# The last layer norm of a decoder layer: statistics by token on partitions, means and affines dealt out anew

## What is computed

```python
def layer_norm(x, g, b):
    mu = mean(x); var = mean((x - mu) ** 2)
    return (x - mu) * rsqrt(var + 1e-5) * g + b

h = silu(x @ w_ffn_gate) * (x @ w_ffn_up)
x = layer_norm(ALPHA * x + h @ w_ffn_down, ln_ffn_g, ln_ffn_b)
```

## Time and profile before

| | us |
|---|---|
| median of 3 runs | 2103.23 (2102.51 to 2103.74) |
| the profiled execution, its own time | 2103.31 |
| its span in the trace | 2101.7 |
| from tile 15 written (end of the last L2242) to the last affine's end | 2086.12 to 2098.58 |
| issue of the last store to the end of the span | 2099.0 to 2101.7 |

### The profile page before, as it was taken

How to read it: one execution, slowest core, us unless ns; L and a number is a source line. 1 busy time by engine, 2 the same in 40 slices (tenths; PEclk the granted TensorE clock), 3 DMA queues, 4 the chain that set the end, 5 groups by cost and what they waited for, 6 DMA issues and landing times.

```text
span 2101.7 us, 47661 instructions
## 1 busy us (share of the span) xinstructions
PE 2082.1 (99%) x17400; PEld 2065.5 (98%) x17400; DVE 1479.6 (70%) x2395; ACT 1117.4 (53%) x1671; POOL 161.8 (8%) x298
## 2 busy tenths in 40 slices
PE   9999999999999999999999999999999999999997
PEld 8999999999999999999999999999999999999997
DVE  8788877888698988544546876977666666545545
ACT  5566556566545545434434565656666665433333
POOL 1000000000002432000000000001111110000000
PEclk9999999999999999999999999999999999999998
DMA  7555555455567998555556575568888887555553
GB/s 279 195 180 180 191 193 185 159 185 188 184 200 236 319 293 281 182 183 180 180 186 204 193 283 194 164 223 285 278 293 286 277 283 256 176 190 182 181 183 110
DMA packets 125362, 451.78 MB, mean 215 GB/s; under 512 B 16056, under 2 KB 16312, under 8 KB 124232
## 3 DMA queue, kind: packets, MB, share of 16 engines
q1 hardware_dynamic: 101232, 366.41, 51.1%
q0 software_dynamic: 24048, 84.20, 12.9%
HBM read 427.87 MB, written 23.99 MB: 215 GB/s over the span
## 4 chain that ended last, share of the span: by engine, by line
PE 94%; DVE 3%; DMA 1%; ACT 1%; issue 0%; SPq 0%; ACTq 0%; POOL 0%; DVEq 0%
PE G L443 26%; PE G L444 26%; PE G L445 26%; PE M L443 4%; PE M L444 4%; PE M L445 4%; DVE sb_wlo L1482 1%; PE M L593 1%; PE M L605 1%; DMA sb_hist<-in_hist 1%; DMA sb_raw<-in_wstream 1%; DVE sb_resid L1770 0%; ACT sb_whi L953 0%; PE M L596 0%; PE M L576 0%
## 5 line engine op out<-in xcount | busy, mean ns | idle before, releaser
L1482 DVE TENSOR_TENSOR sb_wlo<-sb_raw,sb_whi 128x1024 fp32r<-128x1024 f32 x688 | 833.5, 1223 | 553.9 <-ACT sb_whi L953 550.2
L953 ACT ACTIVATE sb_whi<-sb_raw 128x1024 fp32r<-128x1024 f32 x688 | 720.7, 1057 | 733.7 <-PE G L445 612.9
L443 PE MATMUL G<-sb_xH,sb_whi 128*128 128x264 f32 (+1 forms) x3040 | 860.1, 283 | 2.2 <-DVE sb_wlo L1482 1.8
L445 PE MATMUL G<-sb_xH,sb_wlo 128*128 128x264 f32 (+1 forms) x3040 | 858.3, 282 | 0.0
L444 PE MATMUL G<-sb_xL,sb_whi 128*128 128x264 f32 (+1 forms) x3040 | 857.4, 282 | 0.0
L443 PEld LDWEIGHTS G<-sb_xH,sb_whi 128*128 128x128 f32 x3040 | 570.5, 188 | 4.6 <-DVE sb_wlo L1482 2.7
L444 PEld LDWEIGHTS G<-sb_xL,sb_whi 128*128 128x128 f32 x3040 | 570.1, 188 | 0.0
L445 PEld LDWEIGHTS G<-sb_xH,sb_wlo 128*128 128x128 f32 x3040 | 570.0, 188 | 0.0
L443 PE MATMUL G<-sb_hH,sb_whi 128*128 128x264 f32 x704 | 199.5, 283 | 0.0
L444 PE MATMUL G<-sb_hL,sb_whi 128*128 128x264 f32 x704 | 199.3, 283 | 0.0
L445 PE MATMUL G<-sb_hH,sb_wlo 128*128 128x264 f32 x704 | 198.0, 281 | 0.0
(11 more groups left out here) (389 smaller groups left out, 2975.8 us busy)
## 6 DMA issues: line engine op xcount, KB each, us to landing
sb_raw<-in_wstream SPq DMA_DIRECT2D x688, 512.0 KB, 4.2
sb_st<-in_state_ssd POOLq DMA_DIRECT2D x32, 512.0 KB, 6.4
out_new_ssd_s<-sb_st POOLq DMA_DIRECT2D x32, 512.0 KB, 3.9
sb_tmp<-in_state_ssd POOLq DMA_DIRECT2D x34, 256.0 KB, 4.8
...
```

Source lines behind the costliest of these rows:

```text
L443: pe.matmul(out, w, kH, start=start, stop=False)
L445: return pe.matmul(out, wlo[:, slot, at:at + P], kH, start=False, stop=stop)
L953: act.activation(hi, src, ACT.Copy).then_inc(hi_ready, 1)
L1482: dve.tensor_tensor(lo, src, hi.bitcast(F32), ALU.subtract)\
```

## The change

The same sums are made, but the statistics of the last norm lie by token: token on partitions, three columns (tokens 0 to 127, 128 to 255, and the last 128, of which the samples are the last eight rows). So the chain of variance, root and reciprocal runs on 128x3 values. The reciprocals come back to all partitions as a product of ones with a diagonal matrix. In detail:

- PE (`last_sums`): of x the sum to all partitions stays (two matmuls, L756); for both sums there are besides 12 matmuls with a sums tile as the stationary operand and one column of ones as the moving one (`by_token`, L760), each giving 128x1. Where the sum of squares was made for all partitions is nothing now.
- DVE: six operations of 3 or 6 columns (L2305 to L2315), ACT's root on 3 columns (L1480). Then DVE builds the diagonal `rdiag` (128x256 and 128x8, L2316, L2319), PE multiplies (`last_norm`, L787), DVE copies the result from PSUM to SBUF (`RSTD[2]`, L2324). ACT's square of the mean (L1446) is gone.
- Means: DVE takes it from pair 0, POOL from pairs 1 to 5 (five, not four), PE from pairs 6 and 7: the tile times the identity plus the mean times minus the identity, in PSUM (L778, L782).
- `scaled` takes `RSTD[2]` in SBUF as its second operand, and for pairs 6 and 7 the PSUM tiles as its first. The order is 0, 1, 6, 2, 7, 3, 4, 5.
- Affines: ACT has 12 tiles (pairs 0, 1, 6, 2, 7, 3), DVE four (4, 5). The stores go in the order 0, 1, 6, 2, 4, 7, 3, 5.
- One DVE operation more, 128x128, at the start of the last projection (`minus`).
- Five semaphores of the step that makes dt become two counters, `dt_vec` and `dt_act`: waits and increments stay on the same instructions.

```diff
--- before.py
+++ after.py
@@ -212,6 +212,9 @@
 OUT_SETS = (1, 0, 2)
+LAST_BY_ACT = (0, 1, 6, 2, 7, 3)
+LAST_BY_DVE = (4, 5)
+LAST_STORES = (0, 1, 6, 2, 4, 7, 3, 5)
 OUT_PAIRS = (1, 0, 2)
@@ -368,6 +371,8 @@
             outer=([P, 2, XPG, P],))
+        spare = outer[:, :, :, :].rearrange("p b i n -> p (b i n)")
+        rdiag, minus, tok = spare[:, 0:T], spare[:, T:T + P], spare[:, T + P:T + P + 9]
         (cols,) = overlay(2 * UNIT * 4, cols=([P, 2, 2, 2],))
...
@@ -420,12 +425,12 @@
                     load(i * RING, k)
-            for c in range(8):
-                if c < 7:
-                    sp.wait_ge(s["xn_ready"], 16 + c + 1)
+            for p in LAST_STORES:
+                if p in LAST_BY_ACT:
+                    sp.wait_ge(s["xn_ready"], 16 + LAST_BY_ACT.index(p) + 1)
                 else:
-                    sp.wait_ge(s["zn_ready"], 16)
-                sp.dma_start(o["yT"][:, c * 2 * T:(c + 1) * 2 * T], flat(resid[:, 2 * c:2 * c + 2, :]))\
+                    sp.wait_ge(s["zn_ready"], 8 + len(LAST_BY_ACT) + LAST_BY_DVE.index(p) + 1)
+                sp.dma_start(o["yT"][:, p * 2 * T:(p + 1) * 2 * T], flat(resid[:, 2 * p:2 * p + 2, :]))\
                     .then_inc(s["y_out"], 16)
@@ -544,7 +549,7 @@
-                    pe.wait_ge(s["dt_ready"], 1)
+                    pe.wait_ge(s["dt_vec"], 3)
@@ -747,15 +752,43 @@
-                def add(k, tile, start=False, stop=False):
-                    return pe.matmul(STAT[2][k][:, 0:T], ones[:, :], tile, start=start, stop=stop)
-                for k in range(2):
-                    pe.wait_ge(s["dsum_ready"], 4 + k + 1)
-                    add(k, SUMS[2][:, k, 0, :], start=True)
+                def all_rows(tile, start=False, stop=False):
+                    return pe.matmul(STAT[2][0][:, 0:T], ones[:, :], tile, start=start, stop=stop)
+
+                def by_token(out, tile):
+                    for c, at in enumerate((0, P, T - P)):
+                        last = pe.matmul(out[:, c:c + 1], tile[:, at:at + P], ones[:, 0:1], start=True, stop=True)
+                    return last
+
+                pe.wait_ge(s["dsum_ready"], 5)
+                all_rows(SUMS[2][:, 0, 0, :], start=True)
+                by_token(M[1][:, 0:3], SUMS[2][:, 0, 0, :])
+                pe.wait_ge(s["dsum_ready"], 6)
+                by_token(M[1][:, 3:6], SUMS[2][:, 1, 0, :]).then_inc(s["tok_stats"], 1)
                 pe.wait_ge(s["res_ready"], 25)
-                add(0, resid[:, KT - 1, :], stop=True).then_inc(s["ln_sum"], 1)
+                by_token(M[3], resid[:, KT - 1, :]).then_inc(s["tok_stats"], 1)
                 pe.wait_ge(s["dsq_ready"], 25)
-                add(1, SQUARES[2][:, 1, 1, :], stop=True).then_inc(s["ln_sq"], 1)
+                by_token(G[1][1], SQUARES[2][:, 1, 1, :]).then_inc(s["tok_stats"], 1)
+                all_rows(resid[:, KT - 1, :], stop=True).then_inc(s["ln_sum"], 1)
+
+            def last_norm():
+
+                def copied(p):
+                    for j in range(2):
+                        pe.matmul(GP[p - 6][:, j, 0:T], ident[:, :], resid[:, 2 * p + j, :], start=True, stop=False)
+
+                def less_mean(p):
+                    for j in range(2):
+                        last = pe.matmul(GP[p - 6][:, j, 0:T], minus, MEAN[2][:, :], start=False, stop=True)
+                    last.then_inc(s["last_ps"], 1)
+
+                copied(6)
+                pe.wait_ge(s["diag_ready"], 1)
+                pe.matmul(M[2][:, 0:T], ones[:, :], rdiag, start=True, stop=True).then_inc(s["last_ps"], 1)
+                pe.wait_ge(s["mean_ready"], 3)
+                less_mean(6)
+                copied(7)
+                less_mean(7)
@@ -926,6 +959,7 @@
             last_sums()
+            last_norm()
             assert t["unit"].now() == N_UNITS, (t["unit"].now(), N_UNITS)
...
@@ -1442,12 +1476,12 @@
                 act.activation(SQUARES[2][:, 1, j, :], resid[:, KT - 2 + j, :], ACT.Square).then_inc(s["dsq_ready"], 1)
+            act.wait_ge(s["var_ready"], 3)
+            act.activation(tok[:, 3:6], tok[:, 3:6], ACT.Sqrt, bias=eps[:, 1:2]).then_inc(s["lsd_ready"], 1)
             act.wait_ge(s["ln_sum"], 3)
-            act.activation(RSTD[2][:, :], STAT[2][0][:, 0:T], ACT.Square, scale=1.0 / D_MODEL).then_inc(s["mean_ready"], 1)
             act.activation(MEAN[2][:, :], STAT[2][0][:, 0:T], ACT.Copy, scale=1.0 / D_MODEL).then_inc(s["mean_ready"], 1)
-            ln_sd(2)
-            for p in range(7):
-                act.wait_ge(s["zn_ready"], 8 + p + 1)
+            for n, p in enumerate(LAST_BY_ACT):
+                act.wait_ge(s["zn_ready"], 8 + n + 1)
                 for k in (2 * p, 2 * p + 1):
...
@@ -2214,6 +2248,7 @@
             dve.wait_ge(s["st_out1"], 16 * 16)
+            dve.tensor_scalar(minus, ident[:, :], -1.0, None, ALU.mult)
             for b in range(7):
@@ -2254,37 +2289,49 @@
-            def less_mean(p):
-                total = STAT[2][0][:, 0:T].rearrange("p (o t) -> p o t", o=1).to_broadcast([P, 2, T])
-                return mark(dve.scalar_tensor_tensor(out=two(p), in0=total, scalar=-1.0 / D_MODEL, in1=two(p),
-                                                     op0=ALU.mult, op1=ALU.add))
-
-            def scaled(p):
-                return dve.tensor_tensor(two(p), two(p), M[2][:, 0:T].rearrange("p (o t) -> p o t", o=1).to_broadcast([P, 2, T]),
-                                         ALU.mult)
-
-            ln_variance(2)
-            dve.wait_ge(s["mean_ready"], 4)
-            dve.wait_ge(s["res_ready"], 25)
-            less_mean(0)
+            def spread_two(v):
+                return v.rearrange("p (o t) -> p o t", o=1).to_broadcast([P, 2, T])
+
+            def scaled(p, src=None):
+                return dve.tensor_tensor(two(p), two(p) if src is None else src, spread_two(RSTD[2][:, :]), ALU.mult)
+
+            def affine(p):
+                for k in (2 * p, 2 * p + 1):
+                    last = dve.tensor_scalar(resid[:, k, :], resid[:, k, :], vcol("ln_ffn_g", k), vcol("ln_ffn_b", k),
+                                             ALU.mult, ALU.add)
+                last.then_inc(s["zn_ready"], 1)
+
+            dve.wait_ge(s["tok_stats"], 1)
+            step(dve.tensor_scalar(tok[:, 0:6], M[1][:, 0:6], 1.0 / D_MODEL, None, ALU.mult))
+            dve.wait_ge(s["tok_stats"], 2)
+            step(dve.scalar_tensor_tensor(out=tok[:, 0:3], in0=M[3][:, 0:3], scalar=1.0 / D_MODEL, in1=tok[:, 0:3],
+                                          op0=ALU.mult, op1=ALU.add))
+            step(dve.tensor_tensor(tok[:, 6:9], tok[:, 0:3], tok[:, 0:3], ALU.mult))
+            step(dve.tensor_tensor(tok[:, 3:6], tok[:, 3:6], tok[:, 6:9], ALU.subtract))
+            dve.wait_ge(s["tok_stats"], 3)
+            dve.scalar_tensor_tensor(out=tok[:, 3:6], in0=G[1][1][:, 0:3], scalar=1.0 / D_MODEL, in1=tok[:, 3:6],
+                                     op0=ALU.mult, op1=ALU.add).then_inc(s["var_ready"], 1)
             dve.wait_ge(s["lsd_ready"], 3)
-            reciprocal = mark(dve.reciprocal(M[2][:, 0:T], RSTD[2][:, :]))
-            after(reciprocal)
-            for p in range(6):
-                if p == 1:
-                    after(less_mean(1))
-                if p >= 2:
-                    dve.wait_ge(s["centred"], p - 1)
-                scaled(p).then_inc(s["zn_ready"], 1)
-            for p in (6, 7):
-                after(less_mean(p))
-                if p == 6:
-                    scaled(p).then_inc(s["zn_ready"], 1)
-            step(scaled(7))
-            for k in (14, 15):
-                last = dve.tensor_scalar(resid[:, k, :], resid[:, k, :], vcol("ln_ffn_g", k), vcol("ln_ffn_b", k),
-                                         ALU.mult, ALU.add)
-            last.then_inc(s["zn_ready"], 1)
+            step(dve.reciprocal(tok[:, 3:6], tok[:, 3:6]))
+            dve.tensor_tensor(rdiag[:, 0:SEQ].rearrange("p (c n) -> p c n", c=2),
+                              ident[:, :].rearrange("p (o n) -> p o n", o=1).to_broadcast([P, 2, P]),
+                              tok[:, 3:5].rearrange("p (c o) -> p c o", o=1).to_broadcast([P, 2, P]), ALU.mult)
+            dve.tensor_scalar(rdiag[:, SEQ:T], ident[:, P - NSAMP:P], tok[:, 5:6], None, ALU.mult).then_inc(s["diag_ready"], 1)
+            dve.wait_ge(s["mean_ready"], 3)
+            step(dve.scalar_tensor_tensor(out=two(0), in0=spread_two(STAT[2][0][:, 0:T]), scalar=-1.0 / D_MODEL, in1=two(0),
+                                          op0=ALU.mult, op1=ALU.add))
+            dve.wait_ge(s["last_ps"], 1)
+            step(dve.tensor_copy(RSTD[2][:, :], M[2][:, 0:T]))
+            for p in LAST_BY_ACT:
+                if p >= 6:
+                    dve.wait_ge(s["last_ps"], p - 4)
+                elif p:
+                    dve.wait_ge(s["centred"], p)
+                scaled(p, GP[p - 6][:, :, 0:T] if p >= 6 else None).then_inc(s["zn_ready"], 1)
+            for p in LAST_BY_DVE:
```

(31 more changed lines are left out.)

## The result

The changed kernel takes **2105.87 us** (median of 20 runs, 2105.11 to 2106.96), the kernel before beside it 2103.30 (20 runs, 2102.24 to 2103.89): a ratio of 1.0013 [1.0007, 1.0019]. It is 2.6 us slower. That is under the 0.2% taken as a change, but outside the measurement's interval, and the forecast had it 0.3 us faster. The time is rival A's (2106.2).

The account below looks back on a forecast made before the run. PE, busy 2082.1 of 2101.7 us, was taken as the bound, so only the tail could move: 1.34 us won in pairs, 0.99 lost to a later start, 2103.31 - 0.35 = 2102.96, 2103.0 us; range 2101.8 to 2107.2.

Parts of the forecast that it names:

- rival A: Last norm's pairs: DVE with two SBUF operands and POOL reading SBUF exclude each other and alternate; 2106.2 us, chance 0.30.
- Pairs: Multiplications, affines and stores after the first `scaled`: less work on DVE and ACT gives 1.34 us.
- B: Last norm's pairs: POOL's five operations run without a gap and keep DVE out until done; 2107.7 us, chance 0.12.
- The forecast's 0.45: Chance given to the prediction's own sum for the whole kernel, 2103.0 us.
- Statistics by token: Chain from variance to the reciprocal's copy in SBUF: first `scaled` at 2091.39, 0.99 us later than before.
- The rest: Remaining effects: `minus` hidden, dt counters nothing, PE's clock full; at half, the way back costs some 0.3 us more.
- I count its full clock: PE in the tail: it works on with gaps under 1 us, so its clock was assumed full.
- The narrow matmuls: Sums on PE: 24 passes of one-column matmuls, 0.112 us apart, set by weight loads, ending at 2088.76.
- rival C: Sums on PE: one-column matmuls pace like 264 columns, adding 2.6 us ahead of the statistics; 2105.6 us, chance 0.08.
- The unloading of ACT and DVE: Pairs of the last norm: three multiplications with the mean less on DVE, two affines less on ACT, giving 1.34 us.
- the later statistics: Ahead of the first `scaled`: the narrow chain begins later and has a way back and a copy, taking 0.99 us.

Follow-up runs that it names:

- e1: The changed kernel, but the multiplications of pairs 0 to 5 read the factor from PSUM instead of SBUF: 2104.69 us.
- e4: The changed kernel with POOL's five subtractions left out, POOL only counting: 2103.54 us.
- e5: The changed kernel with POOL's five subtractions replaced by five memsets, which write SBUF but read none: 2103.91 us.
- e3: The changed kernel with the factor from PSUM for pairs 0 to 5 and POOL starting only after the diagonal is written: 2103.72 us.
- e8: The changed kernel with PSUM factor for pairs 0 to 5, POOL after the diagonal, and the SBUF copy moved to just ahead of pair 6: 2103.58 us.
- e7: The kernel before with its own 264-column statistics, plus the change's means, order, affines and stores; SBUF factor only for pairs 6 and 7: 2101.47 us.

## Why the prediction was wrong

**The step that failed** is in "Pairs": "DVE's multiplications step by (3.16 - 0.70) / 4 = 0.615 us". That pace had been read where the second operand lay in PSUM. With both in SBUF beside POOL's reading, three `scaled` took 1.73, 1.80 and 1.18 us. DVE's program from the first `scaled` to its last affine became 9.20 us, where e1 has 6.56. Of the 2.64 us the end saw 2.0; the rest was slack behind ACT, which ended last in e1. e1, e4 and e5 each take one reason away (the operand, POOL, POOL's reading), and each comes back to 7.2 us. At the last store this step is 0.65 + 1.34 = 1.99 of the 3.06 us between forecast and trace (15.57 for 12.51); the next miss is the other 1.07.

**Rival A had the mechanism and nearly the size.** It put the last store 2101.85 - 2086.12 = 15.73 us behind tile 15; it was 15.57. Inside it was off: A had four `scaled` wait; in fact L2319 waited first, and three `scaled` after it. A's wait of pair 0 (2091.39 to 2092.45, 1.06 us) is as long as the 1.07 us by which L2319 made the first `scaled` late. That A's time is this near is in part luck. B fell: POOL's operations follow each other without a pause in its program, and still DVE got in after each one it had waited for. The forecast's 0.45 against A's 0.30 rested on no row showing such a pair; that was no evidence, as the text said, and yet it tipped the choice. The Trainium skill (SBUF — State Buffer, section "Who interferes with whom") states that a DVE instruction with two SBUF inputs contends with a GpSimd instruction that reads SBUF and not with one that only writes it. The traces agree: 1.73 and 1.80 us beside the subtraction, at most 0.71 beside the memsets.

**A second miss, in "Statistics by token":** "diagonal of 128x256 2089.50 to 2089.92 (0.417), its samples until 2090.02". The tensor_tensor of 128x256 took its 0.43, but POOL began 0.13 us ahead of the 8-column `tensor_scalar` and held it until its first operation was done: 1.26 us, for 0.23 without POOL beside it (e1 to e4), and the first `scaled` 1.07 us later than forecast. The instruction has only one SBUF tensor, beside one scalar per partition, so rival A, told of two operands, did not cover it. The Trainium skill (SBUF — State Buffer, section "Who interferes with whom") names `tensor_scalar` among the operations that can take the ports shared with GpSimd in their faster modes. L2319's wait and e3's affines agree with it. A faster pace from SBUF is in the trace of before too (groups by line and shape: xcount | busy us, mean ns | idle):

```profile
L1813 DVE TENSOR_SCALAR sb_tmp<-M,sb_vec 128x264 f32<-128x264 f32 x12 | 5.1, 484 | 0.1
...
L2285 DVE TENSOR_SCALAR sb_resid<-sb_resid,sb_vec 128x264 f32<-128x264 f32 x2 | 0.7, 415 | 0.0
```

The first reads its tensor from PSUM and has one scalar per partition, the second reads from SBUF, has two, and is still shorter. What makes L2319 wait is not shown beyond that: its scalar lies in SBUF as well, and no run took the one or the other away.

**A third, in "The rest":** "at half, the way back would cost some 0.3 us more". It cost 0.6 to 1.4 (1.47 to 2.26 less 0.87), since pair 6's passes stand ahead of it on PE and are slowed too. And "I count its full clock" held in the profiled execution, not in six of eight with one-column matmuls. The half clock is the likely reason why e1, e3, e4, e5 and e8 lie 0.7 to 1.2 us over what was expected of them; for e3, whose one profile has the full clock, there is only the spread of its runs to say so.

**The last 0.45 us**, from the last store's issue to the end, was taken as unchanged. It was 2.9 to 3.2 us in every kernel with the new order of stores, 2.7 to 2.8 in the two with the old one. The traces place it in the landing of the last store: 2.8 us from issue to landing in the changed kernel, 2.4 before, with 0.4 us from there to the end in both. Stores issued 1 us or more apart land in 2.0 to 2.1 us in both. The changed kernel's last four go at 2099.34, 2099.71, 2100.19 and 2100.73 and land in 2.1, 2.4, 2.7 and 2.8 us; before, only the last one followed so closely (0.37 us). That the crowding is the cause fits this and was not tried by itself.

**What held.** The narrow matmuls pace by their weight loads, as taken from the earlier trace rows; weight loads of TensorE in the changed kernel:

```profile
2086.20 0.75 PEld L760 LDWEIGHTS M<-sb_ones,sb_resid 128*128 128x128 f32 x6
```

(0.75 - 0.19) / 5 = 0.112 us a pass: rival C fell. The diagonal began 3.39 us behind tile 15 for 2089.50 - 2086.12 = 3.38 forecast, the copy took 0.43 for 0.41. The unloading of ACT and DVE was worth 1.35 us (e7) for 1.34, and the later statistics 1.02 (5.30 in e3 less 4.28) for 0.99. So with the two collisions out, the sum is right to 0.02 us at the last store (e3).
